# Expert weights in 4 MB loads with 32 KB runs, and up-product columns dealt out by fours

## What is computed

```python
logits = h @ router_w + router_b            # 256 tokens, 32 experts, top 4 kept
for e in range(32):                         # the tokens of expert e
    gu = xb @ w_up[e] + b_up[e]             # w_up[e]: 1024 x 2048, 8 MB
    x_glu, x_lin = split(gu)                # each 1024 wide
    act = min(x_glu, 7) * sigmoid(1.702 * x_glu) * (clip(x_lin, -7, 7) + 1)
    y = act @ w_down[e] + b_down[e]         # w_down[e]: 1024 x 1024, 4 MB
    out[tok] += y * gate
```

## Time and profile before

| | us |
|---|---|
| median of 3 runs | 1157.29 (1157.25 to 1157.68) |
| profiled execution | 1156.24 |
| its span | 1154.4 |
| PE busy | 1104.0 (96%) |
| DVE busy | 408.7 (35%) |
| ACT busy | 232.9 (20%) |
| mean rate of the transfers | 388 GB/s over the span, 447.65 MB |

### The profile page before, as it was taken

One profiled execution on the slowest core, in us unless ns is written; L12 is line 12 of the kernel. 1 busy time (PEld: TensorE's weight loads), 2 busy tenths in 40 slices (PEclk: granted clock), 3 DMA queues, 4 the chain that ended last, 5 costly groups with the idle time before them and its releaser, 6 DMA issues.

```text
span 1154.4 us, 14307 instructions
## 1 busy us (share of the span) xinstructions
PE 1104.0 (96%) x5779; PEld 529.0 (46%) x5779; DVE 408.7 (35%) x703; ACT 232.9 (20%) x333; POOL 21.1 (2%) x34
## 2 busy tenths in 40 slices
PE   9999999999999999999999999999999999999997
PEld 8899998433333333333333333333333333333336
DVE  6899997322222221221212222222222222222237
ACT  5645454301100100000100010100000001111027
POOL 2100000000000000000000000000000000000011
PEclk9999999999999999999999999999999999999999
DMA  9985579899999999999999999999999999999991
GB/s 281 354 281 170 183 293 376 310 391 428 427 427 429 427 429 428 428 429 430 427 429 428 428 430 428 428 428 429 429 429 427 428 427 428 427 429 427 426 398 58
DMA packets 57969, 447.65 MB, mean 388 GB/s; under 512 B 4179, under 2 KB 24907, under 8 KB 32747
## 3 DMA queue, kind: packets, MB, share of 16 engines
q1 hardware_dynamic: 56932, 444.44, 93.3%
q0 software_dynamic: 672, 1.99, 0.6%
q10 hardware_dynamic: 327, 0.69, 0.2%
HBM read 446.05 MB, written 1.05 MB: 387 GB/s over the span
## 4 chain that ended last, share of the span: by engine, by line
PE 56%; DMA 39%; ACT 2%; DVE 1%; SPq 1%; issue 1%; POOL 0%; DVEq 0%; ACTq 0%; POOLq 0%
DMA down_ring<-in_expert_w_down_dram 19%; PE ps L2010 17%; DMA up_ring<-in_expert_w_up_dram 16%; PE ps L2051 14%; PE ps L1745 5%; PE ps L2064 3%; PE ps L1935 3%; PE ps L1755 3%; DMA up_ring<-in_ple_gate_w_dram 2%; PE ps L1811 2%; DMA up_ring<-in_w_in_dram 1%; PE ps L1837 1%; PE ps L1816 1%; ACT hT L965 1%; PE ps L2165 1%
## 5 line engine op out<-in xcount | busy, mean ns | idle before, releaser
L2010 PE MATMUL ps<-up_ring,hT 128*64 128x512 f32 x2040 | 447.8, 593 | 11.0 <-DMA up_ring<-in_expert_w_up_dram 10.5
L2010 PEld LDWEIGHTS ps<-up_ring,hT 128*64 128x64 f32 x2040 | 150.1, 137 | 299.5 <-issue 273.5
L2051 PE MATMUL ps<-down_ring,hT 128*64 128x512 f32 x992 | 231.1, 608 | 24.4 <-DMA down_ring<-in_expert_w_down_dram 17.8
L1502 DVE TENSOR_SCALAR extra<-ps 128x512 f32<-128x512 f32 x32 | 22.1, 692 | 506.9 <-PE ps L2021 506.9
L1488 DVE TENSOR_TENSOR x_sb<-x_sb,ps 128x1024 f32<-128x1024 f32 x64 | 78.2, 1221 | 185.3 <-PE ps L2064 178.7
L2051 PEld LDWEIGHTS ps<-down_ring,hT 128*64 128x64 f32 x992 | 68.5, 139 | 163.6 <-issue 140.9
L961 ACT ACTIVATE work<-ps 128x512 f32<-128x512 f32 x31 | 18.5, 597 | 377.2 <-PE ps L2021 377.2
L1745 PE MATMUL ps<-h_hi,w_hi 128*128 128x256 f32 x304 | 74.3, 285 | 2.1 <-ACT up_ring L834 2.1
L1745 PE MATMUL ps<-h_lo,w_hi 128*128 128x256 f32 x304 | 73.8, 283 | 0.0
L2064 PE MATMUL ps<-hT,extra 64*128 64x512 f32 x256 | 72.0, 640 | 0.8 <-DVE hT L1537 0.8
L472 DVE TENSOR_TENSOR w_lo<-up_ring,w_hi 128x2048 fp32r<-128x2048 f32 x28 | 64.0, 2289 | 6.9 <-ACT w_hi L766 6.8
(11 more groups left out here) (312 smaller groups left out, 808.4 us busy)
## 6 DMA issues: line engine op xcount, KB each, us to landing
up_ring<-in_expert_w_up_dram SPq DMA_DIRECT2D x125, 2048.0 KB, 27.0
down_ring<-in_expert_w_down_dram SPq DMA_DIRECT2D x63, 2048.0 KB, 21.5
up_ring<-in_w_in_dram SPq DMA_DIRECT2D x21, 1024.0 KB, 6.8
up_ring<-in_branch_w_dram SPq DMA_DIRECT2D x6, 1024.0 KB, 5.1
up_ring<-in_expert_w_up_dram SPq DMA_DIRECT2D x5, 1024.0 KB, 11.3
up_ring<-in_w_out_dram SPq DMA_DIRECT2D x4, 1024.0 KB, 6.9
up_ring<-in_ple_gate_w_dram SPq DMA_DIRECT2D x4, 1024.0 KB, 25.1
down_ring<-in_expert_w_down_dram SPq DMA_DIRECT2D x2, 1024.0 KB, 21.0
```

What stands on the lines that cost most here:

```text
L1502: nc.vector.tensor_scalar(lin, ps[:, LIN, :], 1.0 + LIMIT, 1.0 - LIMIT, ALU.min, ALU.max).then_inc(lin_ready, 1)
L2010: ins = nc.tensor.matmul(ps[64 * g:64 * g + 64, GLU + side, :], xe[:, j, k % 4, k // 4, :], w[:, D * side + 512 * g:D * side + 512 * (g + 1)],
L2051: last = nc.tensor.matmul(ps[64 * g:64 * g + 64, Y, :], actT[:, r, c, :], down_units[:, c, D * r + 512 * g:D * r + 512 * (g + 1)], start=( ...
```

## The change

- `JOINED_UP` (experts 4 to 29) and `JOINED_DOWN` (3 to 28) name the experts whose weights come in 4 MB loads. `load_up_pair` loads two units at once; a partition's two units are now neighbours in memory (row `h*512 + p*4 + k*2 + r` for unit 2h + k), a run of 32 KB. `load_down_pair` loads both down units (row `p*8 + c*4 + r`), again 32 KB per partition.
- A pair of up is issued when both its units of expert q - 2 have been read; a down load when both units of expert q - 1 have been read. TensorE waits for a pair once, before its first unit.
- Single loads (experts 0 to 3, 30, 31 of up; 0 to 2, 29 to 31 of down) keep 16 KB runs, now 32 KB apart in memory. The order of the loads is nearly the same; at expert 16 the hand-mixed pieces become pairs.
- Since unit c of down now holds rows with `(row // 4) % 2 == c`, the up products' columns go to the two halves of the array by fours (`gated_columns`): each product reads 128 runs of 4 columns (16 bytes), 32 bytes apart, in place of 512 neighbours. The bias products read `b_parts` (bf16) in the same pattern.
- `gather` reads with a step of four columns (16 bytes); `moe_gain` follows.

The core of the diff (the branch for overflow, the rows of the first loads and the last expert's waits are changed alike):

```diff
+JOINED_UP = range(4, N_EXP - 2)
+JOINED_DOWN = range(3, N_EXP - 3)
...
             def load_up(j, c, e):
-                rows = expert_w_up[0, bass.ds(e, 1)].rearrange("a (c p r) n -> p (a c) (r n)", p=P, r=UP_ROWS)
-                sp.dma_start(up_units[:, UP_UNITS * j + c, :], rows[:, c, :]
+                rows = expert_w_up[0, bass.ds(e, 1)].rearrange("a (h p k r) n -> p (a h) k (r n)", p=P, k=2, r=UP_ROWS)
+                sp.dma_start(up_units[:, UP_UNITS * j + c, :], rows[:, c // 2, c % 2, :]
                              ).then_inc(up_loaded[UP_UNITS * j + c], 16)
+            def load_up_pair(j, h, e):
+                first = UP_UNITS * j + 2 * h
+                rows = expert_w_up[0, bass.ds(e, 1)].rearrange("a (h p r) n -> p (a h) (r n)", p=P, r=2 * UP_ROWS)
+                sp.dma_start(up_units[:, first:first + 2, :].rearrange("p s b -> p (s b)"), rows[:, h, :]
+                             ).then_inc(up_loaded[first], 16)
...
+            def load_down_pair(e):
+                rows = expert_w_down[0, bass.ds(e, 1)].rearrange("a (p r) n -> p a (r n)", p=P, r=2 * DOWN_ROWS)
+                sp.dma_start(down_units[:, :, :].rearrange("p s b -> p (s b)"), rows[:, 0, :]
+                             ).then_inc(down_loaded[0], 16)
...
+            def refill_up_pairs(q, j, e, halves=range(2)):
+                for h in halves:
+                    sp.wait_ge(up_used, UP_UNITS * (q - 2) + 2 * h + 2)
+                    load_up_pair(j, h, e)
+            def refill_down_pair(q, e):
+                sp.wait_ge(down_used, DOWN_UNITS * q)
+                load_down_pair(e)
...
             with sp.Fori(2, EARLY_LOADS // 2) as i:
                 for j in range(2):
-                    refill_up(2 * i + j, j, 2 * i + j)
-                    refill_down(2 * i + j - 1, 2 * i + j - 1)
+                    refill_up_pairs(2 * i + j, j, 2 * i + j)
+                    refill_down_pair(2 * i + j - 1, 2 * i + j - 1)
             e = EARLY_LOADS
-            refill_up(e, 0, e)
-            refill_down(e - 1, e - 1)
-            for c in range(DOWN_UNITS):
-                refill_up(e + 1, 1, e + 1, [c])
-                refill_down(e, e, [c])
-            refill_up(e + 1, 1, e + 1, range(DOWN_UNITS, UP_UNITS))
-            for q in range(e + 1, e + 5):
-                refill_up(q + 1, (q + 1) % 2, q + 1, [0])
-                refill_down(q, q)
-                refill_up(q + 1, (q + 1) % 2, q + 1, range(1, UP_UNITS))
-            refill_down(e + 5, e + 5)
-            with sp.Fori(EARLY_LOADS // 2 + 3, N_EXP // 2 - 1) as i:
+            refill_up_pairs(e, 0, e)
+            refill_down_pair(e - 1, e - 1)
+            for q in range(e, e + 5):
+                refill_up_pairs(q + 1, (q + 1) % 2, q + 1, [0])
+                refill_down_pair(q, q)
+                refill_up_pairs(q + 1, (q + 1) % 2, q + 1, [1])
+            refill_down_pair(e + 5, e + 5)
+            with sp.Fori(EARLY_LOADS // 2 + 3, N_EXP // 2 - 2) as i:
                 for j in range(2):
-                    refill_up(2 * i + j, j, 2 * i + j)
-                    refill_down(2 * i + j, 2 * i + j)
+                    refill_up_pairs(2 * i + j, j, 2 * i + j)
+                    refill_down_pair(2 * i + j, 2 * i + j)
+            for q in range(N_EXP - 4, N_EXP - 2):
+                refill_up_pairs(q, q % 2, q)
+                (refill_down_pair if q in JOINED_DOWN else refill_down)(q, q)
...
-                        rows = xs[:, a, 512 * g:512 * (g + 1)].rearrange("p (c n r) -> p c r n", c=2, r=UP_ROWS)
+                        rows = xs[:, a, 512 * g:512 * (g + 1)].rearrange("p (n r) -> p r n", r=2 * UP_ROWS)
...
+            def gated_columns(w, side, g):
+                return w[:, D * side:D * (side + 1)].rearrange("p (n g r) -> p g n r", g=2, r=DOWN_ROWS)[:, g]
...
-                    else:
+                    elif c % 2 == 0:
                         pe.wait_ge(up_loaded[UP_UNITS * j + c], 16 * turn + 16)
+                    elif not joined(q, JOINED_UP):
+                        pe.wait_ge(up_loaded[UP_UNITS * j + c], 16 * single_loads(q, 2, JOINED_UP))
...
                                 ins = nc.tensor.matmul(ps[64 * g:64 * g + 64, GLU + side, :],
                                                        xe[:, j, k % 4, k // 4, :],
-                                                       w[:, D * side + 512 * g:D * side + 512 * (g + 1)],
+                                                       gated_columns(w, side, g),
                                                        start=(k == 0), stop=False)
```

More of the change, by code:

```diff
@@ L524, in load_up @@
             def load_up(j, c, e):
[L525 to L526 removed]
+                rows = expert_w_up[0, bass.ds(e, 1)].rearrange("a (h p k r) n -> p (a h) k (r n)", p=P, k=2, r=UP_ROWS)
+                sp.dma_start(up_units[:, UP_UNITS * j + c, :], rows[:, c // 2, c % 2, :]
                              ).then_inc(up_loaded[UP_UNITS * j + c], 16)
+            def load_up_pair(j, h, e):
[3 more added lines that the diff above has]
+                             ).then_inc(up_loaded[first], 16)
             def load_down(c, e):
[L530 removed]
+                rows = expert_w_down[0, bass.ds(e, 1)].rearrange("a (p c r) n -> p (a c) (r n)", p=P, r=DOWN_ROWS)
                 sp.dma_start(down_units[:, c, :], rows[:, c, :]).then_inc(down_loaded[c], 16)
+            def load_down_pair(e):
+                rows = expert_w_down[0, bass.ds(e, 1)].rearrange("a (p r) n -> p a (r n)", p=P, r=2 * DOWN_ROWS)
+                sp.dma_start(down_units[:, :, :].rearrange("p s b -> p (s b)"), rows[:, 0, :]
+                             ).then_inc(down_loaded[0], 16)
             for u in range(2, MIX_UNITS):
@@ L562, in _ @@
             load_down(0, 0)
-            early_rows = expert_w_up[0, EARLY_EXPERT].rearrange("(c p r) n -> p c r n", p=P, r=UP_ROWS)
+            early_rows = expert_w_up[0, EARLY_EXPERT].rearrange("(h p r) n -> p h r n", p=P, r=2 * UP_ROWS)
             sp.dma_start(early_row, early_rows[:, 0, 0, :]).then_inc(single_rows_loaded, 16)
-            rows = expert_w_up[0, 0].rearrange("(c p r) n -> p c r n", p=P, r=UP_ROWS)
+            rows = expert_w_up[0, 0].rearrange("(h p r) n -> p h r n", p=P, r=2 * UP_ROWS)
             for r in range(UP_ROWS):
@@ L568, in _ @@
                 sp.wait_ge(w_used, OUT_UNIT0 + 1 + r)
-                sp.dma_start(up_ring[:, RAW_SLOT + r, :], rows[:, 2, r, :]).then_inc(landed, 16)
+                sp.dma_start(up_ring[:, RAW_SLOT + r, :], rows[:, 1, r, :]).then_inc(landed, 16)
             sp.dma_start(b_rest[:, :].rearrange("p (c n) -> p c n", c=2),
@@ L590, in load_last_rows @@
                 c = UP_UNITS - 1
-                rows = expert_w_up[0, e].rearrange("(c p r) n -> p c r n", p=P, r=UP_ROWS)
+                rows = expert_w_up[0, e].rearrange("(h p k r) n -> p h k r n", p=P, k=2, r=UP_ROWS)
                 for r in range(UP_ROWS):
                     landed = single_rows_loaded if r == 0 else up_loaded[UP_UNITS * j + c]
-                    sp.dma_start(up_ring[:, 2 * (UP_UNITS * j + c) + r, :], rows[:, c, r, :]).then_inc(landed, 16)
+                    sp.dma_start(up_ring[:, 2 * (UP_UNITS * j + c) + r, :], rows[:, 1, 1, r, :]).then_inc(landed, 16)
             def load_gate():
@@ L605, in load_last_halves @@
                 c, n = DOWN_UNITS - 1, UNIT
-                rows = expert_w_down[0, e].rearrange("(c p r) n -> p c (r n)", p=P, r=DOWN_ROWS)
+                rows = expert_w_down[0, e].rearrange("(p c r) n -> p c (r n)", p=P, r=DOWN_ROWS)
                 for half in range(2):
@@ L655, in _ @@
                             q = N_EXP * r + 2 * i + j
-                            refill_up(q, j, 2 * i + j)
-                            refill_down(q, 2 * i + j)
+                            refill_up_pairs(q, j, 2 * i + j)
+                            refill_down_pair(q, 2 * i + j)
                 sp.wait_ge(up_used, UP_UNITS * ROUNDS * N_EXP)
@@ L701, in _ @@
             pool.dma_start(rb[:, :], on_all(router_b[0])).then_inc(mats_loaded, 16)
-            pool.dma_start(moe_gain[:, :].rearrange("p (c r) -> p c r", r=UP_ROWS),
-                           moe_norm[0].rearrange("(c p r) -> p c r", p=P, r=UP_ROWS)).then_inc(mats_loaded, 16)
+            pool.dma_start(moe_gain[:, :].rearrange("p (h r) -> p h r", h=2),
+                           moe_norm[0].rearrange("(h p r) -> p h r", h=2, p=P)).then_inc(mats_loaded, 16)
             pool.wait_ge(sgu_loaded, 32)
@@ L1962, in _ @@
                     for g in range(2):
-                        rows = xs[:, a, 512 * g + 256 * c:512 * g + 256 * (c + 1)].rearrange("p (n r) -> p r n", r=UP_ROWS)
+                        rows = xs[:, a, 512 * g:512 * (g + 1)].rearrange("p (n c r) -> p c r n", c=2, r=UP_ROWS)[:, c]
                         last = nc.tensor.matmul(ps[64 * g:64 * g + 64, (GATHER, ACTT)[c], 0:256], select[:, 0, a, :],
@@ L1979, in biases_to_tokens, with joined, single_loads @@
                 last.then_inc(comb_done, 1)
```

(13 more changed lines are left out.)

4 lines of the change are left out of this document (2 added, 2 removed).

## The result

Before: 1157.68 us, median of 5 runs (1157.25 to 1159.04). The changed kernel: **1181.83 us**, median of 5 (1180.45 to 1183.97). The ratio is 1.0207, 95% interval 1.0192 to 1.0222: slower, by 24.2 us. The forecast was 1153.8 with a range to 1162.0; the prediction's rival 3, with a price of 14.5 us, is the one that happened. All ratios leave out slow executions, of which there was one, of 3965 us, among the 12 of the kernel with single loads at the end. The profiled execution took 1183.97 for a span of 1182.2, the longest of its runs: its token-mixing stage, ahead of the experts and untouched by the change, ended 4.2 us later than in the kernel before (the router's products start at 208.45, not 204.29; in the ten other traces at 204.6 to 207.6).

What follows compares the result with a forecast made beforehand. The prediction took the weight transfers at 428 GB/s to set the pace. Its terms, -5.5 for longer runs, +0.8 and +0.8 for holes, +0.4 for the gather, sum to -3.5: 1157.3 becomes 1153.8 us, range 1151.0 to 1162.0.

Steps and rivals of the forecast that it cites:

- rival 3: Gather: one column per 16-byte line runs at half pace, some 860 ns per pair; +14.5 us, near 1172; chance 0.15.
- Part 3 (a): Gather's step of 16 bytes instead of 8: 0.14 us per expert on TensorE, 0.4 us in the sum.
- Part 1: Joined loads: 624 runs per engine saved at 8.8 ns each, 5.5 us saved (bounds 3.3 and 7.7).
- Part 2: Weight stream: coarser loads are issued later, leaving a hole of 0.8 us at each of two order changes.
- the ledger: Account of L, the work queued when a down load goes out; it gave both holes of 0.8 us.
- The start: First joined loads, up pair and down of expert 3: issued just in time, 0 us (bound 0.6).
- Part 3 (b): Up products reading 16-byte runs, 32 apart: 0 us, upper bound 0.67 us per expert.
- rivals 2 and 4: Up products: spaced runs cost 0.67 us per expert (chance 0.2); jumps between runs cost 28 us per expert (chance 0.02).
- Rival 1: Joined loads: chip doesn't reward runs over 16 KB, only the holes stay: +2.0, 1159.3 us; chance 0.15.
- (c): Bias products, the gain's load and single loads with 32 KB pitch: 0; bias at most 0.2 us per expert, hidden.
- (d): Expert loop: TensorE's waits on second halves go; they were free when passed, no size given.
- The end: Tail: TensorE ends its last expert 0.5 us closer to the gate weights' landing, within its 0.68 us wait there.

Runs made afterwards that it cites:

- the gather mended: Changed kernel with the 16-byte step moved from the gather to the transposes of the gathered rows, gather reading neighbours: 1158.99 us, ratio 1.0007.
- the covered kernel: Kernel with the step in the transposes, with single loads for up of experts 28, 29 and down of 15, 16, 20, 21: 1155.14 us, ratio 0.9970.
- the scan: Kernel before with other gather read patterns in nine experts, run once: 430 to 918 ns per pair.

## Why the prediction was wrong

The step that failed is **Part 3 (a)**, the price of the gather's 16-byte step. It was put at 0.14 us per expert with an upper bound of 1.0, from the transposes of the activation; it is 3.60 - 1.80 = 1.80 in the chain and 1.81 in the expert's period, 13 times what was taken. Of 57.9 us in all, TensorE's waits hid 28.3. The row that I leaned on was of the stationary operand. There the same step costs 64 ns per load of 128 columns and hides beside the matmuls; as the moving operand, 512 columns wide, it halves the pace of the array. The upper bound was no bound: it too was built from the stationary row. The case stood in the prediction as rival 3, with 860 ns for a pair (900 measured), and got 0.15 because of that one pace.

**Rival 3's own sum** was too low, 14.5 where 24.2 was measured. Its p of 28.5 was near (28.75). It kept the loads as the base, -5.5, and added TensorE's delays to it. In the trace TensorE is the base. The kernel before ran seven experts at 26.9 us on a queue that goes at 29.4 before its first wait: 7 x 2.5 = 17 us of weights stood in stock. At 28.75 against 29.1 only 0.4 per expert is drawn from that, 9 us by expert 25 (an estimate from these periods), and the four experts with the projection, at 30.8, put some back. Added up as TensorE's work it gives 23.6. The two holes of rival 3, 1.7 and 6.7, were near (2.5 and 6.7 in the windows above) but are no cost: the kernel before with the new gather has 3.5 and 0.4 there (shares of 0.90 and 0.99 in the same 35 us) and takes the same time from the router on, 973.3 us against 973.8.

**Part 1**, longer runs, -5.5: right, if on the low side. An expert at the loads' pace takes 29.13 us where it took 29.36: 0.23 us over 24 runs saved, 9.6 ns a run (8.8 was taken). In the traces the median 32 KB run takes 1213 to 1215 ns where two of 16 KB take 1226, 11 to 13 ns. Windows of 58 us show 430 to 433 GB/s; and the coarse loads without long runs, against the same with them, give 5.8 to 7.3 us.

**Part 2**, holes: place right, both changes of order. Size 0.8 each, measured 1.8 and 0.7 at the best and 2.9 and 2.5 where TensorE had just lost time to its clock, which the ledger left out. The start, taken as 0, was right with the gather mended: between 236 and 248 us the share of the transfers is 0.88 to 0.91, before 0.91, a difference of 0.4 us at most.

**Part 3 (b)**, up products free: right, 13.73 us for the 64 products of an expert as before, and with it rivals 2 and 4 fall. Rival 1 falls by the coarse loads without long runs, which go at 428. (c): the bias products take 0.45 us instead of 0.43, nothing seen beyond that, nor of (d). **The end**: "0.5 us closer, within the 0.68" was wrong once the gather is mended. The gain at the gate, 1.95 us, was lost since TensorE was as late as before.

With the gather mended, the forecast of -3.5 would still have met 1159.0, beside 1158.0 for the kernel before: the holes and TensorE's lateness ate it. Without the holes, 3.0 to 3.8 us less than before was measured (1155.14 against 1158.14, 1155.11 to 1155.56 against 1158.95).

## What to carry to other kernels

Price an access pattern by a row of the same operand side: what a weight load hides, a moving operand pays in full. When a layout makes runs longer, look at every reader of it, also those that read another tensor in the same order, and put the stride into the narrowest stationary one. And join loads only where the queue holds more than the wait for the whole place; around a change of order keep them small.

## What the hardware showed besides

The moving side of an fp32 matmul of 512 columns pays by 16-byte lines: 430 ns a pair with four columns to a line, 450 with two, 900 with one, 918 with one in every second line. This was measured with two products side by side on the two halves of the array.

The joined loads make TensorE wait in lumps, and stretches at the 1.2 GHz level follow them. Where TensorE waits for the down weights in the covered kernel (timeline, then windows):

```profile
577.92 5.35 PE L2090 MATMUL ps<-down_ring,hT 128*64 128x512 f32 x16 [2.54 <-DMA down_ring<-in_expert_w_down_dram]
```

```profile
574.50:577.90 3.40, 0.88 (x8) 0.69 (x6) 1.50 (x2) 0.60 (x1) 0.00 (x0) 1.00 0.99 424
578.10:581.30 3.20, 3.20 (x8) 0.79 (x8) 0.00 (x0) 0.00 (x0) 0.00 (x0) 0.50 0.93 399
581.50:585.00 3.50, 3.50 (x18) 0.96 (x16) 0.62 (x1) 0.38 (x1) 0.00 (x0) 1.00 0.98 421
```

TensorE is idle for 2.5 us, then 3.4 us run at 0.50 of its clock, then at 1.00 again: 1.7 us of work lost. A stretch in the kernel before reads the same:

```profile
453.80:457.00 3.20, 2.81 (x8) 0.96 (x10) 0.00 (x0) 0.00 (x0) 0.00 (x0) 0.50 1.01 430
```

Ten of the twelve profiled executions have waits for weights. In the expert loop the kernel before has three such stretches, the scan three, the one with only the up loads joined four, and the seven joined ones five to seven. All 53 lie at a wait of TensorE of over 1.9 us (1.97 to 3.37; 2.41 or 2.42 in the kernel before) that ends within 1.5 us of the stretch's start; 24 more waits of that size have none. There are five such waits in the kernel before and seven to ten with joined loads. The two executions with the slow gather, in which TensorE never waits for weights, have no stretch in the loop. In the middle of the loop the loads' pace hides the loss: the expert with the stretch takes some 30.8 us and the next 27.5, together two periods of 29.1. Just ahead of a change of order the stretch widens a hole, as above. In the experts with the projection TensorE has little to win it back with, 28.87 us of its own work against 29.13. That the lumps bring the stretches about was not tried by itself; it is what the traces have in common. Nor was it settled how the 8.6 us of the coarse loads without long runs divide: its holes hold 5.2 of it, and what the rest is was not shown; its last bias products end 9.3 us later from the router on than those of the kernel before.
